# Chunk stage of a hybrid decoder layer: exponent arguments computed in three 32-row groups, four loaded and two transposed chunks, output transposes in another place

## The chip, the cores and the metric

The kernel runs on one core of a Trainium2 chip. The metric is device time in microseconds (us) of one execution. Lower is better. Each number quoted as "the time" is the median of three runs. The trace is of one further execution, taken with the hardware profiler.

## The reference, cut to what matters

Two layers (`DEPTH = 2`) of a decoder trunk with 1024 tokens and width 1024. Each layer has one input projection, three mixers that read it (mLSTM, sparse attention, Mamba-2 SSD), one output projection, and a SwiGLU FFN. The change concerns the stage that computes the mLSTM and the SSD mixer. Their recurrences are, per chunk of tokens:

```
# mLSTM, 4 heads of 64
log_d = where(causal, b[t] - b[s] + i[s], -inf)
s   = (q @ k.T) * exp(log_d - m_t)
num = s @ v + scale * (q @ C);  den = sum(s) + scale * (q @ n)
h   = num / max(|den|, exp(-m_t))
C   = decay * C + (w * k).T @ v ;  n = decay * n + sum(w * k)

# SSD, 8 heads of 64, state 128, 2 groups
seg    = where(causal, acum[t] - acum[s], -inf)
scores = (C_t @ B_s.T) * exp(seg)
y      = scores @ (x * dt) + (C @ state) * exp(acum)
state  = state * exp(a_last) + B.T @ (w * x * dt)
out    = rms_norm((y + d_skip * x) * silu(z))          # per group of 256
```

All operands are float32.

## The kernel before, in words

The kernel walks over the chunk stage in NT = 8 chunks of P = 128 tokens, in each of the two layers. All five engines run hand-written instruction lists, one block for each engine, and every ordering between engines is a semaphore wait (`pe.wait_ge(*rowed(...))`). There is no scheduler: the order in the source is the order on each engine, and a waiting instruction holds everything behind it on its engine.

A chunk c goes through these steps. The names are those of the code.

1. SP loads 20 tiles of 128x128 (1280 KB) from DRAM into `wc[c % 3]`. For c >= 3 it waits until chunk c-3 is wholly finished (`chunk_done`).
2. PE transposes 14 of these tiles into PSUM banks 0, 1, 2 and 0 again (`turns`, 4+4+4+2 tiles). ACT copies each bank into `rw` or `vaug` (`rows`), three places deep. The transposes wait until the exponentials of chunk c-1 have been read out of the same banks (`m_exp`, `s_exp`).
3. PE computes the arguments of the 12 exponentials (8 SSD heads, 4 mLSTM heads), `arguments`. For each of three banks there is one 128x512 bf16 matmul, which writes the causal mask, and then four selection matmuls that spread a row of `arow` (8 rows used) or `mrow` (4 rows used) over 128 partitions. A float32 matmul is two instructions in the trace, so `x8` in a row means four matmuls. The three banks go one after the other, and each ends with its own signal.
4. ACT takes 8 exponentials into `pss` and 4 into `pm` (`exps`). Both tiles exist once. So the exponentials of chunk c+1 wait until PE has used those of chunk c (`m_num`, `s_y`).
5. PE computes the products q.k and B.C (`products`), the contributions of the states (`m_inter`, `s_inter`), the updates of the states (`m_upd`, `s_upd`), and the two sums over a chunk (`m_num`, `s_y`). DVE combines them, updates the states and normalises. POOL scales the transposed rows.
6. The finished 128x768 output is transposed back (`turn_m` two tiles, `turn_s` four tiles), one chunk late: PE does it for chunk c-1 in the iteration of chunk c. ACT and DVE split it into the high and low halves `act_hi` and `act_lo` (`hi`, `lo`), which the next stage reads.

In `products` the q.k matmuls take rows 0-63 for one head and rows 64-127 for the next, and write two different banks. The banks for the q.k sums, the outputs and the rest alternate by chunk (`swing`).

In the input projection, long before this stage, ACT writes `arow` from a PSUM bank (`gate_rows`). The stage after it is the output projection. It begins in a new block, when all engines are through the chunk stage.

Of the kernel before, what the change touches and what calls it, by code (L numbers as in the profile page):

```python
# [30 lines left out]
P = 128  # L31
# [5 lines left out]
PLACES = 3  # L37
assert (NT - 2) % PLACES == 0
HALF = 512
HD = 64  # L40
# [56 lines left out]
def constant_table():  # L97
# [11 lines left out]
    for h in range(8):  # L109
        t[h, K_SEL + P * h:K_SEL + P * (h + 1)] = 1.0  # L110
# [10 lines left out]
def build(nc, x, positions, norm_w, w_in, gate_b, m_norm_w, conv_w, conv_b, dt_bias, a_log, d_skip, s_norm_w,  # L121
# [6 lines left out]
    with ctx:  # L128
# [71 lines left out]
        rw = [bb(f"rw{s}", [P, 12, P]) for s in range(PLACES)]  # L200
        vaug = [bb(f"vaug{s}", [P, MH, HD + 1]) for s in range(PLACES)]
# [160 lines left out]
        for L in range(DEPTH):  # L362
# [38 lines left out]
            with nc.Block() as block:  # L401
# [92 lines left out]
                def _(act):  # L494
# [693 lines left out]
            b_clear = sig("b_clear", PLACES + 2)  # L1188
            chunk_done = sig("chunk_done", NT)
# [7 lines left out]
            args = sig("args", 3 * NT)  # L1197
# [28 lines left out]
            hi_s = sig("hi_s", NT)  # L1226

# [20 lines left out]
            x_rows = lambda c: heads(rw[c % PLACES][:, 0:4, :].rearrange("p a b -> p (a b)"), HD)  # L1248
            flat = lambda a: a.rearrange("p a b -> p (a b)")

            with nc.Block() as block:
                @block.sync
                def _(sp):
# [5 lines left out]
                    for c in range(PLACES, NT):  # L1259
                        sp.wait_ge(*chunk_done(L, c - PLACES + 1))  # L1260
                        sp.dma_start(wc[c % PLACES][:, :, :], by_token[:, :, c * P:(c + 1) * P]).then_inc(chunk_in[c % PLACES].sem, 16)

                @block.gpsimd
                def _(pool):
                    for s in range(PLACES):
# [4 lines left out]
                    for c in range(NT):  # L1270
                        s = c % PLACES
# [21 lines left out]
                def _(pe):  # L1293
                    pe.wait_ge(*b_clear(L, PLACES + 2))

                    def turns(c):

                        w = wc[c % PLACES]
                        pe.wait_ge(*chunk_in[c % PLACES](L, 16 * (c // PLACES) + 16))
                        for b, js in enumerate(((0, 1, 2, 3), (4, 5, W_MK, W_MK + 1), (8, 9, 10, 11), (W_MV, W_MV + 1))):  # L1300
                            if b == 0 and c:
                                pe.wait_ge(*m_exp(L, c))
                            if b in (1, 2) and c:
                                pe.wait_ge(*s_exp(L, 2 * c - 2 + b))
                            if b == 3:
                                pe.wait_ge(*rowed(L, 4 * c + 1))
                            for i, j in enumerate(js):
                                mm = pe.transpose(bank(b % 3)[:, i * P:(i + 1) * P], w[:, j], ident)
                            mm.then_inc(turned.sem, 1)

                    def arguments(c):
# [3 lines left out]
                        for b in range(3):  # L1315
                            pe.wait_ge(*rowed(L, 4 * c + (2, 3, 4)[b]))
                            dst = bank((1, 2, 0)[b])
                            pe.matmul(dst.rearrange("p (h n) -> p h n", n=P), below[:, :], four(unit_b[:, :] if b < 2 else minus_b[:, :]),
                                      start=True, stop=False)
                            for h in range(4):  # L1320
                                if b < 2:
                                    mm = pe.matmul(dst[:, h * P:(h + 1) * P], cst[0:SH, K_SEL + P * (4 * b + h):K_SEL + P * (4 * b + h + 1)],
                                                   arow[0:SH, now], start=False, stop=(h == 3))
# [670 lines left out]
```

## Time and profile before

| what | value |
|---|---|
| time, median of 3 runs | 3206.84 us (3204.69 to 3207.92) |
| profiled execution, its own time | 3207.77 us |
| span from first to last instruction of it | 3206.0 us |
| PE busy | 2945.3 us, 92% of the span, 13396 matmul instructions |
| DVE busy | 1238.8 us, 39% |
| ACT busy | 913.0 us, 28% |
| POOL busy | 923.5 us, 29% |
| mean granted TensorE clock | 0.943 |
| DMA | 207.15 MB, mean 65 GB/s |

The kernel is bound by PE over most of its span. The shares are averages over stages of different kinds: projections and FFN are long rows of 128x512 matmuls at full clock, and the chunk stage is a net of short instructions on all engines. The granted clock is told in parts of 2.4 GHz, and takes the levels 1.00 (2.4 GHz) and 0.50 (1.2 GHz); a value in between is a mean over the stretch. Busy PE is not PE at its peak, since a matmul that streams 64 columns counts as busy just as one that streams 512.

### The profile page before, as it was taken

The page shows a single profiled execution, that of the slowest core. Times are in us where ns is not written, and L with a number is a line of the kernel's source. Part 1 is how long each engine was busy: PE and PEld are TensorE (multiplying, and loading weights), DVE is VectorE, ACT ScalarE, POOL GpSimd, SP SyncE. Part 2 cuts the span into 40 slices and gives each one's busy share as a digit, 9 for nine tenths or more (in the row PEclk, how much of TensorE's full clock was granted, in tenths as well). Part 3 has the DMA queues.
Part 4 walks back from the last instruction along what each step waited for, and adds up shares of the span by engine and source line. Part 5 has one row for each costly group of instructions (what it writes and reads, how often), then busy time and mean ns, then how long its engine had stood idle before and what let it go on. Part 6 is the DMA issues. An engine that isn't in the chain of part 4 may idle for free. (4 is left out here: it accounts for less than half of the span.)

```text
span 3206.0 us, 34381 instructions
## 1 busy us (share of the span) xinstructions
PE 2945.3 (92%) x13396; PEld 2351.7 (73%) x13396; DVE 1238.8 (39%) x2196; ACT 913.0 (28%) x1588; POOL 923.5 (29%) x470
## 2 busy tenths in 40 slices
PE   2999999897899999999939999998888999999997
PEld 1767877775778888888727678777667788888885
DVE  3359964463302111221333599545532111122114
ACT  3235434343311111111232354344432111111112
POOL 0127510223123223322311375103231322332223
PEclk9999999777999999999959999998789999999998
DMA  5102310323211111111241023103232111111113
GB/s 183 34 20 63 109 60 14 86 66 118 74 52 53 39 46 46 53 52 39 102 123 34 23 70 110 55 14 96 57 125 68 58 40 46 46 53 52 39 48 123
DMA packets 234143, 207.15 MB, mean 65 GB/s; under 512 B 20448, under 2 KB 208864, under 8 KB 233840
## 3 DMA queue, kind: packets, MB, share of 16 engines
q1 hardware_dynamic: 228272, 184.69, 19.0%
q10 hardware_dynamic: 5760, 20.97, 1.7%
q8 instruction: 70, 1.15, 0.1%
q14 instruction: 41, 0.34, 0.0%
HBM read 166.85 MB, written 42.99 MB: 65 GB/s over the span
## 5 line engine op out<-in xcount | busy, mean ns | idle before, releaser
L1910 PE MATMUL ps<-act_hi,whi 128*128 128x512 f32 x1408 | 552.0, 392 | 19.8 <-POOL wlo L1817 14.5
L1910 PE MATMUL ps<-act_lo,whi 128*128 128x512 f32 x1408 | 551.3, 392 | 0.0
L1910 PE MATMUL ps<-act_hi,wlo 128*128 128x512 f32 x1408 | 551.0, 391 | 0.0
L1944 DVE TENSOR_TENSOR hf<-sg,ps 128x1024 f32<-128x1024 f32 x44 | 53.7, 1221 | 931.7 <-PE ps L1910 931.7
L757 PE MATMUL ps<-act_hi,whi 128*128 128x512 f32 x960 | 395.2, 412 | 5.5 <-DVE act_lo L956 4.7
L757 PE MATMUL ps<-act_lo,whi 128*128 128x512 f32 x960 | 377.8, 394 | 0.0
L757 PE MATMUL ps<-act_hi,wlo 128*128 128x512 f32 x960 | 377.5, 393 | 0.0
L1129 DVE TENSOR_SCALAR_CACHE_REDUCE ties<-score,kth 128x384 uint8<-128x384 f32 (+5 forms) x396 | 348.4, 943 | 4.8
L1817 POOL TENSOR_TENSOR wlo<-raw,whi 128x1024 fp32r<-128x1024 f32 x84 | 200.3, 2396 | 499.6 <-ACT whi L1854 499.6
L1910 PEld LDWEIGHTS ps<-act_hi,whi 128*128 128x128 f32 x1408 | 266.5, 189 | 77.1 <-issue 21.4
L1950 DVE TENSOR_TENSOR yacc<-yacc,ps 128x1024 f32<-128x1024 f32 x176 | 214.8, 1220 | 264.1 <-PE ps L1924 264.1
L1910 PEld LDWEIGHTS ps<-act_lo,whi 128*128 128x128 f32 x1408 | 266.5, 189 | 56.0
L1910 PEld LDWEIGHTS ps<-act_hi,wlo 128*128 128x128 f32 x1408 | 266.3, 189 | 55.8
L1924 PE MATMUL ps<-dhi,hhi 128*128 128x512 f32 x704 | 276.5, 393 | 12.8 <-POOL dlo L1817 11.7
L1924 PE MATMUL ps<-dhi,hlo 128*128 128x512 f32 x704 | 276.0, 392 | 0.0
L1924 PE MATMUL ps<-dlo,hhi 128*128 128x512 f32 x704 | 276.0, 392 | 0.0
L458 POOL TENSOR_TENSOR wlo<-raw,whi 128x1024 fp32r<-128x1024 f32 x58 | 142.2, 2451 | 462.6 <-ACT whi L504 462.6
L1860 ACT ACTIVATE sg<-ps 128x1024 f32<-128x1024 f32 x44 | 45.1, 1026 | 738.2 <-PE ps L1910 738.2
L757 PEld LDWEIGHTS ps<-act_hi,whi 128*128 128x128 f32 x960 | 182.2, 190 | 85.7 <-issue 41.9
L757 PEld LDWEIGHTS ps<-act_hi,wlo 128*128 128x128 f32 x960 | 182.2, 190 | 39.9
L757 PEld LDWEIGHTS ps<-act_lo,whi 128*128 128x128 f32 x960 | 182.5, 190 | 35.4 <-issue 1.9
L1822 POOL TENSOR_TENSOR hlo<-hf,hhi 128x1024 fp32r<-128x1024 f32 x44 | 105.6, 2401 | 356.4 <-ACT hhi L1864 356.4
(289 smaller groups left out, 4115.1 us busy)
## 6 DMA issues: line engine op xcount, KB each, us to landing
raw<-in_w_in SPq DMA_DIRECT2D x56, 512.0 KB, 3.8
raw<-in_w_gate SPq DMA_DIRECT2D x44, 512.0 KB, 3.7
raw<-in_w_up SPq DMA_DIRECT2D x44, 512.0 KB, 3.8
raw<-in_w_down SPq DMA_DIRECT2D x44, 512.0 KB, 3.5
proj_scratch<-stage ACTq DMA_DIRECT2D x40, 512.0 KB, 2.7
wc<-proj_scratch SPq DMA_DIRECT2D x16, 1280.0 KB, 6.5
tap<-out SPq DMA_DIRECT2D x16, 512.0 KB, 3.5
xres<-out SPq DMA_DIRECT2D x16, 512.0 KB, 3.4
```

The costliest lines, as they stand in the source:

```text
L458: pool.tensor_tensor(wlo[u % 2][:, :], src, whi[u % 2][:, :].bitcast(F32), ALU.subtract)\
L757: mm = pe.matmul(ps[:, half, :], w[:, k], a[:, k, cols], start=(k == 0 and m == 0), stop=(k == KT - 1 and m == 2))
L1129: v.tensor_scalar(tie(c), of(c), at(kth, c), 0.0, op, ALU.add, accum_out=at(held, c))
L1817: pool.tensor_tensor(lo_t[s][:, :], raw[s][:, :], hi_t[s][:, :].bitcast(F32), ALU.subtract)\
L1822: pool.tensor_tensor(hlo[p][:, j], hf[:, :], hhi[p][:, j].bitcast(F32), ALU.subtract).then_inc(h_lo.sem, 1)
L1860: act.activation(sg[:, :], unit_psum(0), ACT.Silu).then_inc(silu.sem, 1)
L1910: mm = pe.matmul(ps[:, 2 * s + half, :], w[:, k], a[:, k, cols], start=(k == 0 and m == 0), stop=(k == KT - 1 and m == 2))
L1924: mm = pe.matmul(ps[:, 4 + 2 * (t % 2) + half, :], h[p][:, j, rows], w[j][:, cols], start=(j == 0 and m == 0), stop=(j == 1 and m == 2))
L1944: v.tensor_tensor(hf[:, :], sg[:, :], unit_psum(1), ALU.mult).then_inc(hidden.sem, 1)
L1950: v.tensor_tensor(yacc[:, t], yacc[:, t], turn_bank(t), ALU.add).then_inc(y_add.sem, 1)
```

## The change

- `PLACES = 4`: four chunks are loaded ahead instead of three. The load of chunk c waits for `gated` of chunk c-4, which is the last reader of `wc`, in place of `chunk_done`. `ROWS = 2`: the transposed rows `rw` and `vaug` have two places instead of three.
- The arguments of a chunk: `arow` now holds the SSD rows twice (partitions 0-7 and 32-39) and the mLSTM rows at partitions 64-67. The selection constants lie at the same three offsets. The three mask matmuls come first, then twelve selection matmuls that go round the three banks and the three row groups. There is one signal at the end instead of three. ACT writes the two extra copies once in each layer, in `gate_rows`.
- The transposes of chunk c+1 use two banks (0 and 1) instead of three, and are split: 8 tiles after `s_inter`, 6 tiles after `m_num`. Bank 2 takes the SSD output transposes (`turn_s`), which now stand between them, ahead of the last 6 tiles and of `s_y`, instead of after the arguments.
- ACT and DVE follow the new order: `to_hi_s` between the second and third row copy, `to_hi_m` last, `to_lo_s` after the update of the SSD state and ahead of the mLSTM sum.

```diff
-PLACES = 3
+PLACES = 4
+ROWS = 2
...
-        t[h, K_SEL + P * h:K_SEL + P * (h + 1)] = 1.0
+        for r0 in (0, 32, 64):
+            t[r0 + h, K_SEL + P * h:K_SEL + P * (h + 1)] = 1.0
...
                     def gate_rows():
+                        act.activation(arow[32:32 + SH, :], bank[0:SH, :], ACT.Copy)
                         act.activation(arow[0:SH, :], bank[0:SH, :], ACT.Copy).then_inc(aux_free[s].sem, 1)
                         act.wait_ge(*rows_v(L, 11))
+                        act.activation(arow[64:64 + MH, :], mrow[0:MH, :], ACT.Copy)
...
-                        sp.wait_ge(*chunk_done(L, c - PLACES + 1))
+                        sp.wait_ge(*gated(L, c - PLACES + 1))
...
-                    def turns(c):
+                    def turns(c, b):
...
+                        if b == 0 and c:
+                            pe.wait_ge(*m_exp(L, c))
+                        if b == 1 and c:
+                            pe.wait_ge(*s_exp(L, 2 * c - 1))
+                        if b >= 2:
+                            pe.wait_ge(*rowed(L, 4 * c + b - 1))
+                        for i, j in enumerate(js):
+                            mm = pe.transpose(bank(b % 2)[:, i * P:(i + 1) * P], w[:, j], ident)
...
-                        for b in range(3):
-                            pe.wait_ge(*rowed(L, 4 * c + (2, 3, 4)[b]))
...
+                        pe.wait_ge(*rowed(L, 4 * c + 4))
+                        if c >= 2:
+                            pe.wait_ge(*lo_s(L, c - 1))
+                        for b in (1, 2, 0):
+                            pe.matmul(tiles(bank(b)), below[:, :], four(unit_b[:, :] if b else minus_b[:, :]), start=True, stop=False)
+                        for h in range(4):
+                            for b, r0, n, k in ((1, 0, SH, h), (2, 32, SH, 4 + h), (0, 64, MH, h)):
+                                mm = pe.matmul(bank(b)[:, h * P:(h + 1) * P], cst[r0:r0 + n, K_SEL + P * k:K_SEL + P * (k + 1)],
+                                               arow[r0:r0 + n, now], start=False, stop=(h == 3))
+                        mm.then_inc(args.sem, 1)
...
                     def turn_s(c, b):
                         pe.wait_ge(*s_out(L, c + 1))
-                        pe.wait_ge(*gated(L, c + 1))
+                        if c + 1 < NT:
+                            pe.wait_ge(*s_exp(L, 2 * c + 4))
...
-                        if c:
-                            pe.wait_ge(*chunk_done(L, c - 1))
+                        if c >= 2:
+                            pe.wait_ge(*gated(L, c - 1))
...                                                     # after s_inter
+                        if c + 1 < NT:
+                            load_in(c + 1)
+                            turns(c + 1, 0)
+                            turns(c + 1, 1)
...                                                     # after turn_m
-                        if c + 1 < NT:
-                            turns(c + 1)
...                                                     # after m_num
+                        if c:
+                            turn_s(c - 1, 2)
+                        if c + 1 < NT:
+                            turns(c + 1, 2)
+                            turns(c + 1, 3)
...                                                     # after s_y
                             arguments(c + 1)
-                        if c:
-                            turn_s(c - 1, near)
...                                                     # ACT, after finish(c - 1)
-                            rows(c + 1)
+                            rows(c + 1, 0)
+                            rows(c + 1, 1)
                         if c:
-                            hi(c - 1, swing(c)[0])
+                            to_hi_s(c - 1)
+                        if c + 1 < NT:
+                            rows(c + 1, 2)
+                            rows(c + 1, 3)
+                        if c:
+                            to_hi_m(c - 1)
...                                                     # DVE, after the update of smem
+                        if c:
+                            to_lo_s(c - 1)
...                                                     # DVE, last in the iteration
-                            lo(c - 1, near)
+                            to_lo_m(c - 1)
```

PE's list in the middle of the chunk stage, one iteration, before. Here `cst,wc` are the transposes of loaded tiles, `cst,catr` those of outputs, `pss`, `pm` the exponentials, and the last eight rows are the arguments, `turn_s` and the products:

```order
L1381 MATMUL ps<-vaug,wk 128x130 x2
L1386 MATMUL ps<-xw,rw 128x256 x2
L1350 MATMUL ps<-cst,catr 128x128 x2
L1308 MATMUL ps<-cst,wc 128x128 x14
L1396 MATMUL ps<-vaug,pm 128x65 x4
L1402 MATMUL ps<-xdt,pss 128x64 x8
L1318 MATMUL ps<-unit_b,below 128x512
L1322 MATMUL ps<-arow,cst 128x128 x4
L1318 MATMUL ps<-unit_b,below 128x512
L1322 MATMUL ps<-arow,cst 128x128 x4
L1318 MATMUL ps<-minus_b,below 128x512
L1325 MATMUL ps<-mrow,cst 128x128 x4
```

The same place on PE with the change (the line numbers are those of the changed kernel, L1314 the transposes of loaded tiles, L1353 `turn_m`, L1362 `turn_s`):

```order
L1314 MATMUL ps<-cst,wc 128x128 x8
L1391 MATMUL ps<-vaug,wk 128x130 x2
L1396 MATMUL ps<-xw,rw 128x256 x2
L1353 MATMUL ps<-cst,catr 128x128 x2
L1404 MATMUL ps<-vaug,pm 128x65 x4
L1362 MATMUL ps<-cst,catr 128x128 x4
L1314 MATMUL ps<-cst,wc 128x128 x6
L1415 MATMUL ps<-xdt,pss 128x64 x8
L1325 MATMUL ps<-unit_b,below 128x512 x2
L1325 MATMUL ps<-minus_b,below 128x512
L1328 MATMUL ps<-arow,cst 128x128 x12
```

Eight transposes moved ahead of the state updates. `turn_s` moved from behind the arguments to ahead of the last six transposes. The three pairs of mask and selection matmuls became one run of three and one run of twelve.

ACT's list between the finish of a chunk and the next exponentials, before (L1467 writes the normalised SSD output, L1427 are the copies of the transposed rows, L1474 and L1476 the high halves of mLSTM and SSD, L1437 the SSD exponentials):

```order
L1467 ACTIVATE catr<-y,small 128x256 x2
L1427 ACTIVATE rw<-ps 128x512 x3
L1427 ACTIVATE vaug<-ps 128x4x64
L1474 ACTIVATE act_hi<-catf 128x2x128
L1476 ACTIVATE act_hi<-ps 128x4x128
L1437 ACTIVATE pss<-ps,scol_minus 128x128 x8
```

The same place on ACT with the change (L1474 the normalised output, L1437 the row copies, L1484 and L1480 the high halves of SSD and mLSTM, L1445 the exponentials):

```order
L1474 ACTIVATE catr<-y,small 128x256 x2
L1437 ACTIVATE rw<-ps 128x512 x2
L1484 ACTIVATE act_hi<-ps 128x4x128
L1437 ACTIVATE rw<-ps 128x512
L1437 ACTIVATE vaug<-ps 128x4x64
L1480 ACTIVATE act_hi<-catf 128x2x128
L1445 ACTIVATE pss<-ps,scol_minus 128x128 x8
```

The high half of the SSD output moved from the last place before the exponentials to a place among the row copies.

## Rows read from the trace of the kernel before

**Rows 1.** Windows: both chunk stages, then one period of layer 1 and of layer 0.

```profile
core 0: us, PE busy (x) PEld busy (x) DVE busy (x) ACT busy (x) POOL busy (x), PEclk, DMA share, GB/s
572.40:731.30 158.90, 139.31 (x792) 115.92 (x792) 86.95 (x199) 68.10 (x225) 40.55 (x45) 0.75 0.28 73
2167.00:2319.80 152.80, 131.06 (x792) 109.71 (x792) 87.55 (x199) 67.76 (x225) 40.46 (x43) 0.80 0.28 76
2192.22:2206.32 14.10, 14.10 (x98) 12.25 (x97) 9.74 (x24) 7.98 (x27) 4.89 (x5) 0.88 0.00 1
614.88:634.15 19.27, 18.07 (x101) 14.83 (x101) 10.76 (x26) 8.25 (x28) 4.89 (x5) 0.73 0.26 69
```

**Rows 2.** Timeline (start, us, what): first mask matmul of chunks 0 and 7, both layers.

```profile
581.90 0.63 PE L1318 MATMUL ps<-unit_b,below 128*128 128x512 bf16 x1
...
708.90 0.38 PE L1318 MATMUL ps<-unit_b,below 128*128 128x512 bf16 x1
...
2176.79 0.38 PE L1318 MATMUL ps<-unit_b,below 128*128 128x512 bf16 x1
...
2296.34 0.38 PE L1318 MATMUL ps<-unit_b,below 128*128 128x512 bf16 x1
```

**Rows 3.** Timeline of PE, chunk 1 to 2 of layer 1.

```profile
2200.59 0.61 PE L1381 MATMUL ps<-vaug,wk 128*128 128x130 f32 x4
2201.04 1.03 PE L1386 MATMUL ps<-xw,rw 128*128 128x256 f32 x4
...
2202.12 1.73 PE L1308 MATMUL ps<-cst,wc 128*128 128x128 f32 x14
2203.69 1.00 PE L1396 MATMUL ps<-vaug,pm 128*128 128x65 f32 x8
2204.53 1.95 PE L1402 MATMUL ps<-xdt,pss 128*128 128x64 f32 x16
2206.32 0.38 PE L1318 MATMUL ps<-unit_b,below 128*128 128x512 bf16 x1
2206.63 1.15 PE L1322 MATMUL ps<-arow,cst 8*128 8x128 f32 x8
...
2210.52 0.89 PE L1358 MATMUL ps<-cst,catr 128*128 128x128 f32 x4
```

**Rows 4.** PE's waits (total us, times, longest), chunk stage of layer 0, then 1.

```profile
PE ps L1308 <- DMA wc<-proj_scratch: 14.5, 6, 7.6
...
PE ps L1308 <- DMA wc<-proj_scratch: 14.9, 6, 8.3
```

**Rows 5.** Timeline of PE, selections and q.k products of chunk 2, layer 0.

```profile
618.99 2.07 PE L1325 MATMUL ps<-mrow,cst 4*128 4x128 f32 x8
...
622.04 1.23 PE L1337 MATMUL ps<-wc 64*128 64x128 f32 x8
```

**Rows 6.** Windows with the clock at either level, layer 0.

```profile
600.00:609.00 9.00, 9.00 (x38) 7.46 (x38) 3.70 (x9) 5.09 (x20) 0.32 (x1) 0.50 0.00 0
610.00:613.00 3.00, 3.00 (x27) 2.82 (x26) 1.66 (x5) 1.68 (x4) 1.25 (x2) 1.00 0.00 0
```

**Rows 7.** Timeline of ACT, layer 1, exponentials and the normalised SSD output.

```profile
2229.42 2.16 ACT L1437 ACTIVATE pss<-ps,scol_minus 128x128 f32<-128x128 f32 x8
2231.42 1.20 ACT L1443 ACTIVATE pm<-ps,gcol 128x128 f32<-128x128 f32 x4
...
2234.25 0.91 ACT L1467 ACTIVATE catr<-y,small 128x256 f32<-128x256 f32 x2
```

**Rows 8.** Timeline of DVE, layer 1, low half and the next products.

```profile
2229.56 0.69 DVE L1521 TENSOR_TENSOR act_lo<-ps,act_hi 128x512 fp32r<-128x512 f32 x1 [2.42 <-ACT act_hi L1476]
2231.62 1.29 DVE L1533 TENSOR_TENSOR pss<-pss,ps 128x512 f32<-128x512 f32 x2 [1.37 <-ACT pss L1437]
```

**Rows 9.** Timeline of ACT, layer 0, the copy of `arow` in the projection.

```profile
145.12 1.02 ACT L658 ACTIVATE arow<-ps 8x1024 f32<-8x1024 f32 x1 [0.82 <-PE ps L798]
...
150.78 0.60 ACT L548 ACTIVATE stage<-ps 128x512 f32<-128x512 f32 x1 [4.55 <-PE ps L757]
```

More of the change, by code:

```diff
@@ L1226, in build @@
             hi_s = sig("hi_s", NT)
+            lo_s = sig("lo_s", NT)
             U_WO = N_PROJ
@@ L1264, in _ @@
                 def _(pool):
-                    for s in range(PLACES):
+                    for s in range(ROWS):
                         pool.memset(vaug[s][:, :, HD:HD + 1], 1.0).then_inc(b_clear.sem, 1)
@@ L1314, in arguments @@
                         four = lambda a: a.rearrange("p (o n) -> p o n", o=1).broadcast_to([P, 4, P])
-                        for b in range(3):
-                            pe.wait_ge(*rowed(L, 4 * c + (2, 3, 4)[b]))
[L1317 to L1323, printed above, removed]
-                                else:
-                                    mm = pe.matmul(dst[:, h * P:(h + 1) * P], cst[0:MH, K_SEL + P * h:K_SEL + P * (h + 1)],
-                                                   mrow[0:MH, now], start=False, stop=(h == 3))
-                            mm.then_inc(args.sem, 1)
+                        pe.wait_ge(*rowed(L, 4 * c + 4))
[8 more added lines that the diff above has]
+                        mm.then_inc(args.sem, 1)
                     def products(c):
@@ L1359, in turn_s @@
                         mm.then_inc(cat_s.sem, 1)
-                    turns(0)
+                    load_in(0)
+                    for b in range(4):
+                        turns(0, b)
                     arguments(0)
@@ L1412, in _ @@
                     turn_m(NT - 1, near)
-                    turn_s(NT - 1, 7)
+                    pe.wait_ge(*lo_s(L, NT - 1))
+                    turn_s(NT - 1, 2)
                 @block.scalar
@@ L1469, in finish, with to_hi_m, to_hi_s @@
                         ins.then_inc(s_out.sem, 1)
-                    def hi(c, b):
-                        now = slice(c * P, (c + 1) * P)
+                    def to_hi_m(c):
                         act.wait_ge(*gated(L, c + 1))
-                        act.activation(act_hi[:, 0:2, now], catf[:, :, :], ACT.Copy).then_inc(hi_m.sem, 1)
+                        act.activation(act_hi[:, 0:2, c * P:(c + 1) * P], catf[:, :, :], ACT.Copy).then_inc(hi_m.sem, 1)
+                    def to_hi_s(c):
                         act.wait_ge(*cat_s(L, c + 1))
-                        act.activation(act_hi[:, 4:8, now], tiles(bank(b)), ACT.Copy).then_inc(hi_s.sem, 1)
-                    rows(0)
+                        act.activation(act_hi[:, 4:8, c * P:(c + 1) * P], tiles(bank(2)), ACT.Copy).then_inc(hi_s.sem, 1)
+                    for b in range(4):
+                        rows(0, b)
                     for c in range(NT):
@@ L1519, in lo, with to_lo_s @@
                         v.tensor_tensor(act_lo[:, 0:2, now], catf[:, :, :], act_hi[:, 0:2, now].bitcast(F32), ALU.subtract)
+                    def to_lo_s(c):
+                        now = slice(c * P, (c + 1) * P)
                         v.wait_ge(*hi_s(L, c + 1))
-                        v.tensor_tensor(act_lo[:, 4:8, now], tiles(bank(b)), act_hi[:, 4:8, now].bitcast(F32), ALU.subtract)\
-                         .then_inc(chunk_done.sem, 1)
+                        v.tensor_tensor(act_lo[:, 4:8, now], tiles(bank(2)), act_hi[:, 4:8, now].bitcast(F32), ALU.subtract)\
+                         .then_inc(lo_s.sem, 1)
                     for c in range(NT):
-                        s = c % PLACES
+                        s = c % ROWS
                         near, far = swing(c)
```

64 lines of the change are left out of this document (26 added, 38 removed).

## The prediction

> **What bounds the kernel now.** I read the page first (PE busy 92%), and then went to the stage that the change touches, by windows of time, since the share is a mean over unlike stages. The two chunk stages take 158.9 and 152.8 us of the span [rows 1], together 311.7 us or 10%. The reader is to see three things there: PE is busy 86 to 88% of it, DVE 55 to 57%, ACT 43 to 44%, so PE is the bound; and PE has a granted clock of 0.75 and 0.80, where the whole span has 0.943. Second, from the starts of the first mask matmul of chunks 0 and 7 the period of a chunk is (708.90 - 581.90)/7 = 18.1 us in layer 0 and (2296.34 - 2176.79)/7 = 17.1 us in layer 1 [rows 2], 17.6 in the mean. Third, PE waits for the loads of `wc`: 14.5 and 14.9 us in 6 waits each [rows 4]. One of the six is the start of the stage (7.6 and 8.3); the five others are 6.9 and 6.6 us.
>
> PE's own work in a period at full clock: the shortest period, 2192.22 to 2206.32, has PE busy all its 14.10 us at a mean clock of 0.88 [rows 1]. So 0.24 of it, 3.4 us, ran at half the clock, which cost 1.7 us, and 12.4 is left; it is the one period without `turn_s`, which adds 0.5. Sum 12.9. The parts of it, from start to start [rows 3]: `m_upd` 0.45 (0.55 where it doesn't follow closely), `s_upd` 0.87, `turn_m` 0.21, 14 transposes 1.57, `m_num` 0.84, `s_y` 1.79, the arguments 2206.32 to 2210.52 = 4.20; products and state contributions are the rest, 2.5. The mean period is 17.6, so 4.7 us go to the low clock and to waits, 0.96 of them (13.5/14) to the `wc` loads.
>
> The low clock is tied to the arguments. The granted clock is 0.50 from 600 to 609 and 1.00 from 610 to 613 [rows 6]. It falls while PE works through selections that use 8 or 4 of the 128 rows, and within a period never in a stretch of transposes and full-row products. In most chunks it falls during or just behind the selections, and stays low through the products and state contributions.
>
> **The change part by part.**
>
> *Arguments.* Before: three times a mask (0.31) and eight selection instructions (1.09, that is 8 x 0.112 and a gap of 0.2 [rows 3]; the third bank as the first). Now the eight of one bank run beside the eight of the other two, if row groups run side by side. What the trace shows of that: at the low clock eight selections on the same rows take 2.07 us, and the eight q.k instructions, alternating between rows 0-63 and 64-127 and between two banks, take 1.23 for the same 128 columns each [rows 5]. Less the tail of one instruction (0.4 to 0.5) that is 0.21 and 0.11 for each: pairs run fully side by side. For three groups I take the same: 8 rounds x 0.112 = 0.87. Masks: 0.31 + 2 x 0.22 = 0.75 (512 bf16 columns, no change of rows between them). Exit 0.2. Sum 1.8 against 4.2 at full clock: 2.4 us less. Bounds: not side by side at all, 24 x 0.109 + 0.2 + 0.75 = 3.6 (0.6 less); below 1.8 nothing, since one group's 0.87 must pass.
>
> The Trainium skill (TensorE: Matmul & The Clock Gate, "Measured speedup vs the span model") gives 3.07x for four row tiles rather than 4x. By this share three groups give 2.3x, an estimate of 1.14 us in place of 0.87, and the whole time would be some 4 us longer than by the row. I stay with the row, and the range has room for the other.
>
> *Clock.* The stretch of few-row work shrinks from 3 x 1.09 with masks between them to one of 1.1 us. In layer 1 a stretch with one run of eight selections at its end (2204.5 to 2207.7: `s_y`, mask, selections) kept full clock (those selections take 1.15 us [rows 3], against 2.07 at the low clock [rows 5]). So I expect the clock to stay at 1.00 from about the second chunk on. Bounds: mean clock as now (0.78), or 1.00.
>
> The Trainium skill says of PE transposes (same page, "Part 4: PE-mode transpose") that the full clock "doesn't engage" for them. By that rule the change, which puts more transposes next to the selections, would lose clock; but 610 to 613 holds the 14 transposes and stands at 1.00 [rows 6], so the measurement speaks against it. What it would give is the second rival.
>
> *Loads of `wc`.* Chunk c is asked for when chunk c-4 is gated, that is more than a period before PE needs it, and lands in 6.5 us (page, part 6): the 13.5 us of waits go. The fourth load stands ahead of two weight loads that are needed only in the next stage: nothing. The first chunk still has to land.
>
> *Two banks for the transposes.* At the start of the stage banks 2 and 3 of the turn must wait for row copies of 0.6 each (the 128x512 copy in [rows 9] is of this shape), and the arguments wait for all four copies: 0.8 us later per layer.
>
> *Copies in `gate_rows`.* Two of 1.02 us, behind them ACT is idle 4.55 us [rows 9]. Nothing; without that cover 2 us per layer.
>
> *The new period.* With PE faster, the ring through ACT decides. From the end of the arguments: signal 0.1; twelve exponentials 2.0 + 1.2 = 3.2 [rows 7]; then eight transposes, which wait for them, 0.95 (DVE is done with `pm` at about the same time: 2.2 for the SSD exponentials, then 1.2 for its products [rows 8] and 0.7 for the two half as long); then on PE without a wait `m_upd` 0.55, `s_upd` 0.87, `turn_m` 0.21, `m_num` 0.84, `turn_s` 0.5, six transposes 0.67, `s_y` 1.79 = 5.4; arguments 1.8; semaphores 0.2. Sum 11.7. The SSD output that `turn_s` needs is ready 5.9 us in (2229.42 to 2235.16 is 5.7 [rows 7]), ahead of `turn_s` at about 7.1. PE alone needs 12.9 - 2.4 = 10.5 and is idle 1.2 us. DVE is busy 10.76 us in a period [rows 1] and now waits in `to_lo_s` for ACT's high half, about 0.6 us, with the mLSTM sum and its eight followers queued behind: 11.4. Two rings that nearly tie make each other late, so I take 11.9. Bounds: DVE's busy time alone, 10.8 or rounded 11.0; above, 13.0 with the 3.07x rule and a lost microsecond.
>
> *Sum.* Stage now: 9.5 to the first arguments (581.90 - 572.40) + 0.8; seven periods 83.3; a clock that is low in the first chunk 1.0; from the last arguments to the end 19.5 (now 731.3 - 708.9 = 22.4 and 23.5; the arguments there save 3.3, and the rest of it, a chain through DVE and ACT, stays). Together 114.1 us. Saved 158.9 - 114.1 = 44.8 and 152.8 - 114.1 = 38.7, in all 83.5 us. The profiled execution took 3207.8 (span 3206.0 and 1.8 around it): 3207.8 - 83.5 = 3124.3. It lies 0.9 above the median of the runs shown, so 3123.4; rounded 3124.
>
> **The rivals.**
>
> *First: three groups don't run side by side.* The trace shows two halves only, not thirds, and the selections have 8 and 4 rows. Then arguments cost 3.6, PE's work is 12.3, the ring is 13.5, and the clock falls as now, which takes 0.6 more: 14.1 (the shortest period of today [rows 1]). 14 x (17.6 - 14.1) = 49, less 1 at the start: 3160.
>
> *Second: side by side, but the clock goes on falling in each chunk.* For it: the waits of PE in the new ring (1.2 us) and more transposes; against it: [rows 6]. With the clock of today, 0.78, PE's 10.5 become 13.5, and with the wait, which shortens, 14.3 at most: 14 x 3.3 = 46 saved, 3161; with 0.88 it is 10.5/0.88 + 1.2 = 13.1, 63 saved, 3144.
>
> *Third, the other side: slower.* If the idle time in the ring keeps the clock at 0.50 through the stage, PE's list is 2 x 10.5 less what doesn't scale (`s_y` and `m_num`, bound by loading weights, about 2.6) = 18.4, and with what is left of the wait 18.8: 14 x (18.8 - 17.6) = 17 longer, 3224. It decides once the period is over 17.6, a mean clock under about 0.55. Against it: even today's chunks with 1.4 us of wait for `wc` come back to 1.00.
>
> *Fourth: a new wait eats the gain.* A load or the single signal of the arguments (ACT used to start after the first bank, 2.8 us ahead of the third) holds ACT. The signal is in the ring above already; only a wait of 5 us per chunk would take the gain, and I find none.
>
> **How the numbers follow.** Forecast 70%, its own range 3108 (period 11.0, 12.6 us less, and 3 more in the ends) to 3140 (period 13.0). First rival 9% (3150 to 3170), second 14% (3140 to 3165), slower 4%, no change 3%. The range reaches from 3108 to 3158 and leaves out about 2 in 10. A measurement of this kernel tells 0.2% (6.4 us) from no change: faster 0.93, same 0.03, slower 0.04.
>
> **What would show it.** Stages of about 114 us each, at a clock near 0.95; a period of 11.9. The selections as one run of 24 instructions in 1.1 to 1.2 us at full clock. No wait of PE for `wc` but the first. Waits of PE for ACT's `pm` of about 1 us in each chunk, and DVE waiting about 0.6 us for `act_hi` of the SSD. It would be wrong if the 24 instructions take over 2.5 us, if the clock in the stage stays under 0.9, or if PE waits over 1 us for `lo_s` or the row copies ahead of the masks.

## The result and the profile after

| | before | changed |
|---|---|---|
| time, us (median of 4 runs) | 3207.01 (3204.69 to 3207.92) | 3123.11 (3122.56 to 3123.50) |
| ratio, 95% interval | | 0.9739 [0.9724, 0.9753] |
| span of the profiled execution | 3206.0 | 3121.3 |
| granted clock over the span | 0.943 | 0.954 |

The changed kernel is 84 us faster. From the head of its page: PE's busy time fell, its share stayed at 92%, and the work of the other engines is as before. (One run of one kernel below, at 3408 us with a granted clock of 0.83 over its span, is left out of that kernel's median.)

```profile
PE 2857.1 (92%) x13396; PEld 2280.2 (73%) x13396; DVE 1243.5 (40%) x2196; ACT 916.2 (29%) x1592; POOL 921.2 (30%) x468
```

The windows of both chunk stages and of one period (they answer to [rows 1]; columns as there):

```profile
573.20:684.70 111.50, 89.48 (x792) 75.78 (x792) 87.91 (x199) 67.20 (x225) 39.20 (x42) 0.93 0.40 105
2119.40:2235.00 115.60, 93.40 (x792) 78.89 (x792) 88.15 (x199) 67.44 (x225) 39.41 (x44) 0.88 0.38 101
618.41:630.31 11.90, 10.88 (x101) 9.29 (x99) 11.18 (x26) 8.24 (x28) 4.86 (x6) 1.00 0.40 106
```

The stages took 158.9 and 152.8 us and take 111.5 and 115.6: 47.4 + 37.2 = 84.6, the whole gain. What lies ahead of, between and behind them is unchanged to 1 us. In the period DVE is now busy 11.18 of 11.90 us and PE 10.88: the bound has moved from PE to DVE. The clock, 0.73 to 0.88 in the two periods of before, is 1.00 in this one. Over the stages it is 0.93 and 0.88, since it is low at their start and end.

The timeline of PE over one period of layer 0 (start, us; answers to [rows 3]):

```profile
611.48 1.06 PE L1314 MATMUL ps<-cst,wc 128*128 128x128 f32 x8 [0.88 <-ACT pm L1450]
612.67 0.71 PE L1391 MATMUL ps<-vaug,wk 128*128 128x130 f32 x4
613.23 1.03 PE L1396 MATMUL ps<-xw,rw 128*128 128x256 f32 x4
614.09 0.38 PE L1353 MATMUL ps<-cst,catr 128*128 128x128 f32 x2
614.31 1.00 PE L1404 MATMUL ps<-vaug,pm 128*128 128x65 f32 x8
615.15 0.61 PE L1362 MATMUL ps<-cst,catr 128*128 128x128 f32 x4
615.59 0.82 PE L1314 MATMUL ps<-cst,wc 128*128 128x128 f32 x6
616.25 1.90 PE L1415 MATMUL ps<-xdt,pss 128*128 128x64 f32 x16
617.98 0.59 PE L1325 MATMUL ps<-unit_b,below 128*128 128x512 bf16 x2
618.41 0.38 PE L1325 MATMUL ps<-minus_b,below 128*128 128x512 bf16 x1
618.72 1.17 PE L1328 MATMUL ps<-arow,cst 8*128 8x128 f32 x24
619.82 0.71 PE L1340 MATMUL ps<-wc 64*128 64x128 f32 x8
```

The arguments take 619.82 - 617.98 = 1.84 us, against 4.20 [rows 3]. The 24 selections take 1.10 from their start to the next instruction; less 0.2 of exit that is 0.90, eight rounds of 0.112. Their bar in the timeline is 1.17 long, where that of eight selections alone was 1.15 [rows 3]. The same holds at the low clock, which the first chunk of layer 1 shows: 2.08 for 24, where eight alone took 2.07 [rows 5].

```profile
2132.25 2.08 PE L1328 MATMUL ps<-arow,cst 8*128 8x128 f32 x24
```

PE now has two gaps: 0.88 us for ACT's `pm`, and about 0.3 between those eight transposes and `m_upd` (612.67 - 611.48 = 1.19, where the two follow each other at 0.90 in the second period, 599.92 to 600.82). The wait for `pm` is new, PE did not have it before; `wc` is now waited for once (waits of PE in layer 0: total, times, longest; the first line answers to [rows 4]):

```profile
PE ps L1314 <- DMA wc<-proj_scratch: 8.0, 1, 8.0
PE ps L1314 <- ACT pm L1450: 6.1, 7, 0.9
```

DVE and POOL over the same period, from their timelines:

```profile
611.87 0.75 DVE L1557 TENSOR_TENSOR pm<-pm,ps 128x256 f32<-128x256 f32 x2
...
616.42 0.69 DVE L1540 TENSOR_TENSOR act_lo<-ps,act_hi 128x512 fp32r<-128x512 f32 x1 [0.35 <-ACT act_hi L1484]
...
618.55 1.15 DVE L1591 TENSOR_TENSOR hsq<-nd 128x256 f32<-128x256 f32 x1
...
623.77 0.75 DVE L1557 TENSOR_TENSOR pm<-pm,ps 128x256 f32<-128x256 f32 x2
```

```profile
618.23 1.19 POOL L1285 TENSOR_TENSOR xdt<-rw,scol 128x512 f32<-128x512 f32 x1 [1.69 <-PE ps L1415]
```

DVE waits once, 0.35 us for `act_hi`, and from there to the end of the next `pm` it has no wait, only small gaps between instructions that need each other's result. One instruction is longer than its like: the square `hsq` (two operands in SBUF) takes 1.15 us while POOL's product `xdt` runs beside it, and 0.42 where it does not (in the first and last chunk of each layer).

### The profile page after: what moved, and what is told of

Its sections match the earlier page's. It is cut to its first block and busy times, and to the rows that moved or that the text cites. A ratio compares the mean times of both kernels' runs of the same rounds, so it can differ in the third digit from the quotient of the medians.

```text
span 3121.3 us, 34397 instructions
## 1 busy us (share of the span) xinstructions
PE 2857.1 (92%) x13396; PEld 2280.2 (73%) x13396; DVE 1243.5 (40%) x2196; ACT 916.2 (29%) x1592; POOL 921.2 (30%) x468
## 3 DMA queue, kind: packets, MB, share of 16 engines
q8 instruction: 70, 1.15, 0.2%
## 5 line engine op out<-in xcount | busy, mean ns | idle before, releaser
L1932 PE MATMUL ps<-act_hi,whi 128*128 128x512 f32 x1408 | 551.9, 392 | 19.8 <-POOL wlo L1839 14.5
L1946 PE MATMUL ps<-dhi,hhi 128*128 128x512 f32 x704 | 276.5, 393 | 12.8 <-POOL dlo L1839 11.7
```

The costliest lines, as they stand in the source:

```text
L1932: mm = pe.matmul(ps[:, 2 * s + half, :], w[:, k], a[:, k, cols], start=(k == 0 and m == 0), stop=(k == KT - 1 and m == 2))
L1946: mm = pe.matmul(ps[:, 4 + 2 * (t % 2) + half, :], h[p][:, j, rows], w[j][:, cols], start=(j == 0 and m == 0), stop=(j == 1 and m == 2))
```

## The experiments

All times are medians; before stands for the unchanged kernel, run on the same chip in the same hours: 3206.07 us with the first four, 3202.53 with the next four, 3201.30 with the last four. Ratios are against it. "Period" is the time between first mask matmuls of adjacent chunks.

### The parts of the change apart

**Groups of rows alone.** The kernel before, with the 24 selections in one run on three row groups and one signal; its loads, order and banks are kept.

```diff
-for b in range(3):                     # a bank at a time, all on rows 0 to 7
+pe.wait_ge(*rowed(L, 4 * c + 4))
+for b in (1, 2, 0):
+    pe.matmul(tiles(bank(b)), below[:, :], four(...), start=True, stop=False)
+for h in range(4):
+    for b, r0, n, k in ((1, 0, SH, h), (2, 32, SH, 4 + h), (0, 64, MH, h)):
+        mm = pe.matmul(..., cst[r0:r0 + n, ...], arow[r0:r0 + n, now], ...)
```

> The kernel before, with the arguments in three row groups alone (three loads ahead, order of transposes and outputs as before). Theory (fewer microseconds of few-row work, and so a clock that stays high): arguments 1.8 us in place of 4.2, granted clock of the chunk stages about 0.9, the wait for wc of 1 to 1.5 us per chunk stays, period about 14.3 us, time about 3160 us. Rival (the clock gain comes from the new order of the instructions, the grouping saves only its own 2.4 us per period): clock about 0.78, period 15.2 or more, time 3173 us or more.

Measured: 3155.51 us, ratio 0.9841 [0.9825, 0.9858]. 

```profile
592.00:697.00 105.00, 82.40 (x721) 68.63 (x719) 81.76 (x184) 57.98 (x196) 35.55 (x37) 1.00 0.24 64
```

The clock stays at 1.00 without the new order (0.78 in the kernel before, same window). PE is busy only 78% of that window. This part alone gives 50 us, and PE now waits more: in layer 0 16.7 us for `wc` (14.5 before) and 10.5 us in 7 waits for DVE's `pm` ahead of `m_upd` (1.1 in 3 before).

**Loads alone.** Four places for `wc`, two for its rows, and SP asks for a chunk once chunk c-4 is gated.

```diff
-PLACES = 3
+PLACES = 4
+ROWS = 2
-sp.wait_ge(*chunk_done(L, c - PLACES + 1))
+sp.wait_ge(*gated(L, c - PLACES + 1))
```

> The kernel before, with four loaded chunks, two transposed ones and the load released by gated. Theory: the waits for wc after the first, 13.5 us in all, go, the clock goes on falling in each chunk (0.75 to 0.80): time about 3191 us. Rival (the waits only hid another wait, for row copies or exponentials): 3204 to 3207 us.

Measured: 3188.94 us, ratio 0.9943 [0.9927, 0.9960]: 17 us. PE waits for `wc` only at the start of the stage. The clock goes on falling in each chunk: 0.82 in the window below, where the kernel before has 0.76, and 0.80 for 0.83 in layer 1 (2180 to 2300).

```profile
584.00:700.00 116.00, 113.80 (x708) 96.50 (x707) 75.63 (x170) 54.59 (x183) 35.93 (x36) 0.82 0.28 76
```

**Everything but the row groups.** The changed kernel, with all 24 selections on rows 0 to 7.

```diff
-for b, r0, n, k in ((1, 0, SH, h), (2, 32, SH, 4 + h), (0, 64, MH, h)):
-    mm = pe.matmul(..., cst[r0:r0 + n, ...], arow[r0:r0 + n, now], ...)
+for b, src, n, k in ((1, arow, SH, h), (2, arow, SH, 4 + h), (0, mrow, MH, h)):
+    mm = pe.matmul(..., cst[0:n, ...], src[0:n, now], ...)
```

> The changed kernel, with all twelve selections on rows 0 to 7 (arow) and 0 to 3 (mrow), in the same order over the banks. Theory (the row groups run side by side, and that is what the gain rests on): the run of 24 selection instructions takes 24 x 0.11 = 2.6 us in place of 1.1, the clock falls again in most chunks, period 14 to 14.5, time 3155 to 3160 us. Rival (going round three banks is what makes them quick): no change, 3123 us. Rival (the clock stays high, only the work is longer): period 13.2, time 3142 us.

Measured: 3158.15 us, ratio 0.9847 [0.9830, 0.9863]. Its steady period (641.60 to 655.41) is filled by PE, at a clock of 0.88:

```profile
641.60:655.41 13.81, 13.81 (x102) 12.44 (x102) 11.29 (x26) 8.24 (x28) 5.03 (x5) 0.88 0.35 93
642.34:645.21 2.87, 2.87 (x25) 2.75 (x25) 2.77 (x4) 0.00 (x0) 0.69 (x1) 1.00 0.85 209
646.00:649.00 3.00, 3.00 (x13) 2.82 (x12) 1.67 (x4) 2.97 (x14) 0.00 (x0) 0.50 0.00 0
649.30:650.50 1.20, 1.20 (x12) 1.17 (x11) 1.20 (x4) 1.10 (x6) 0.92 (x1) 1.00 0.00 0
```

The selections, 2.87 us from 642.34 to 645.21, run at full clock; it falls just behind them, although PE never stops, and is back when the eight transposes begin (649.33). With loads and order in place, the row groups are worth 35 us.

### Is it the clock, and what lowers it?

**Selections over all 128 rows, in the kernel before.** `arow` and `mrow` are cleared below their rows, and each selection reads 128 rows in place of 8 or 4: the same number of instructions and columns, the same result, every row of the array in use. (POOL clears the two tiles once per layer, in the projection.)

```diff
-pe.matmul(dst[...], cst[0:SH, ...], arow[0:SH, now], ...)
+pe.matmul(dst[...], cst[:, ...], arow[:, now], ...)
```

> The kernel before, with its selections over all 128 rows: rows that were left out are zero in the constants, and the row tiles are cleared first (two POOL memsets per layer). The number of instructions, columns and their order stay. Theory (the clock falls because the selections use 8 or 4 rows of 128): granted clock in the chunk stages 0.9 or more, no fall behind the arguments, period 16.0 to 16.3, time 3185 to 3190 us. Rival (it falls for the length of the instructions, the waits or the transposes): clock 0.75 to 0.80 as before, time 3207 to 3211 us.

Measured: 3171.62 us, ratio 0.9886 [0.9870, 0.9903], 34 us faster for more rows per matmul.

```profile
584.00:700.00 116.00, 95.98 (x743) 85.45 (x743) 79.59 (x179) 60.46 (x207) 38.06 (x39) 1.00 0.28 77
```

In the same window the kernel before has 0.76. Layer 1 agrees but for one fall: 0.98 from 2180 to 2270, for 0.83 before. That fall, 0.50 from 2227 to 2229, came behind two waits of PE, 1.74 us for DVE's `pm` and 2.19 for `wc`, with 1.8 us of work between them. So the cause of the falls in each chunk is shown: selections that use few rows bring the clock down.

The size was too low in every theory, 17 to 22 us for 34, and not all of the 34 is the clock. At full clock the arguments take 628.56 - 625.24 = 3.32 us here and 4.20 before [rows 3]: the gaps between the mask (128 rows) and the selections (8 or 4 rows) are gone.

```profile
625.24 0.38 PE L1322 MATMUL ps<-unit_b,below 128*128 128x512 bf16 x1
...
628.56 0.60 PE L1362 MATMUL ps<-cst,catr 128*128 128x128 f32 x4
```

That is 0.88 us in each of 16 chunks, up to 14 us (an estimate; the other waits of PE shift too). The expectation left this term out, and what remains, about 20, lies within it.

**The same in the new order.** Everything but the row groups, with selections over 128 rows.

```diff
-mm = pe.matmul(..., cst[0:n, ...], src[0:n, now], ...)
+mm = pe.matmul(..., cst[:, ...], src[:, now], ...)
```

> same_rows with its selections over all 128 rows (the left-out rows are zero, the row tiles are cleared first). Theory (same_rows lost by two things: 1.5 us more of selections per chunk, and a falling clock): the clock stays at 1.00 after the start, the run takes 2.7 us, period about 13.1, time about 3140 us. Rival (the clock plays no part in the loss): 3156 to 3160 us.

Measured: 3141.74 us (median of the three runs left), ratio 0.9810 [0.9778, 0.9841]; period 13.12 at a clock of 1.00. So the 35 us of the row groups are about 19 for running side by side (3141.74 against 3123; 23 by the ratios) and about 16 for the clock (3158.15 against 3141.74; 12 by the ratios). Here the arguments differ little: 3.42 us from the first mask to the products, against 3.61 on few rows. So at most 3 of the 16 are the shorter run, and this pair is the cleaner test of what the clock costs.

**Three row groups, one bank after the other.** The groups stay, but the eight instructions of one stand together.

```diff
-for h in range(4):
-    for b, r0, n, k in ((1, 0, SH, h), (2, 32, SH, 4 + h), (0, 64, MH, h)):
+for b, r0, n, k0 in ((1, 0, SH, 0), (2, 32, SH, 4), (0, 64, MH, 0)):
+    for h in range(4):
```

> The changed kernel, its three row groups kept, but the four selections of one bank and group are issued before those of the next. Theory (matmuls start in the order of the list, so groups run side by side only where neighbours in the list are of different groups): the run of 24 instructions takes about 2.6 us as on the same rows, and the time is that of same_rows, 3155 to 3160 us. Rival (PE looks far enough ahead to start a later group early): 1.1 to 1.5 us, time 3123 to 3129 us.

Measured: 3142.01 us, ratio 0.9813 [0.9788, 0.9838]. Neither theory: the run of 24 lies between (PE's timeline).

```profile
649.16 2.26 PE L1329 MATMUL ps<-arow,cst 8*128 8x128 f32 x24
651.36 0.71 PE L1341 MATMUL ps<-wc 64*128 64x128 f32 x8
```

2.20 us to the next instruction less 0.2 of exit is 2.0, 18 rounds of 0.112 where one after the other takes 24 and side by side 8: as if six of the 24 had overlapped, which would be three at each of the two changes of group (the trace does not show the single ones). On these rows, then, instructions of different groups run side by side where they alternate, and mostly not where eight of one group stand together. The bank alternates along with the group; alternating banks alone is not enough (2.87 us with all on the same rows), and whether groups would run side by side into one bank was not tested. The clock falls again in some periods, behind the longer run:

```profile
640.00:660.00 20.00, 20.00 (x145) 17.87 (x144) 17.14 (x38) 13.76 (x49) 8.90 (x9) 0.85 0.25 67
```

### What sets the new period

The prediction named a ring through arguments, exponentials and PE (11.7) and put DVE behind it (11.4). The trace after suggests DVE. The ring was forecast at 11.7 and taken as 11.9, which is also what was measured, so the time can't tell them apart; other kernels can.

**A mask matmul twice.** 0.22 us more of PE inside the ring through the arguments; DVE's ring goes through another part of PE's list, ahead of which PE has a gap. The extra one writes what the next overwrites.

```diff
+pe.matmul(tiles(bank(1)), below[:, :], four(unit_b[:, :]), start=True, stop=True)
 for b in (1, 2, 0):
```

> The changed kernel, with the mask of bank 1 written twice, 0.22 us more on PE ahead of the selections of each chunk. Theory A (the period is set by a ring through DVE: products with the exponentials, mLSTM update and sum, SSD output, and the arguments have 0.3 us to spare, since PE waits that long for DVE's pm after its transposes): 3123 to 3124.5 us. Theory B, that of the prediction (the ring goes through the arguments and the exponentials): 16 x 0.22 = 3.5 us longer, 3126.5 us.

Measured: 3122.46 us, ratio 0.9754 [0.9733, 0.9776]. The period did not move: first masks of adjacent chunks at 617.80 and 629.70 are 11.90 apart (PE's timeline).

```profile
617.80 0.38 PE L1324 MATMUL ps<-unit_b,below 128*128 128x512 bf16 x1
...
623.42 1.06 PE L1314 MATMUL ps<-cst,wc 128*128 128x128 f32 x8 [0.90 <-ACT pm L1451]
624.40 0.71 PE L1392 MATMUL ps<-vaug,wk 128*128 128x130 f32 x4
...
629.70 0.38 PE L1324 MATMUL ps<-unit_b,below 128*128 128x512 bf16 x1
```

From the eight transposes to `m_upd` (L1392) it is now 0.98 us, against 1.19: the gap has taken the extra matmul. In these periods the ring through the arguments does not decide. In the second period of each layer, 11.56 in the changed kernel, it does: there the mask shows in full, 11.78.

**POOL's `xdt` later.** POOL forms `xdt` after fading `smem`, away from `hsq`: 5.6 us behind the first mask in place of 0.25. Nothing else changes.

```diff
-if c:
-    pool.wait_ge(*s_y(L, c))
-pool.tensor_tensor(xdt[...], x_rows(c), gate_of(scol, c, 3, SH, HD), ALU.mult)...
 pool.wait_ge(*s_inter(L, c + 1))
 ...                                    # fade of smem
+if c:
+    pool.wait_ge(*s_y(L, c))
+pool.tensor_tensor(xdt[...], x_rows(c), gate_of(scol, c, 3, SH, HD), ALU.mult)...
```

> The changed kernel, with POOL's product xdt moved behind the fade of the SSD state. In the changed kernel DVE's square hsq takes 1.15 us instead of 0.42 in each period, while POOL works on xdt. Theory A (DVE sets the period, and a DVE instruction with two operands in SBUF is held up by the POOL product beside it): hsq goes back to 0.42 and the period falls by 0.3, where the ring through the arguments takes over: 3118 to 3120 us, less if another DVE instruction is held up instead. Theory B (the arguments set the period): 3123 us, no change, although hsq is shorter.

Measured: 3119.34 us, ratio 0.9742 [0.9720, 0.9764], period 11.57 (619.69 to 631.26). From the timeline:

```profile
619.69 0.59 PE L1325 MATMUL ps<-unit_b,below 128*128 128x512 bf16 x2
620.26 0.42 DVE L1591 TENSOR_TENSOR hsq<-nd 128x256 f32<-128x256 f32 x1
621.74 2.18 ACT L1445 ACTIVATE pss<-ps,scol_minus 128x128 f32<-128x128 f32 x8 [2.57 <-PE ps L1328]
623.95 1.28 DVE L1552 TENSOR_TENSOR pss<-pss,ps 128x512 f32<-128x512 f32 x2 [0.30 <-ACT pss L1445]
625.09 1.06 PE L1314 MATMUL ps<-cst,wc 128*128 128x128 f32 x8 [0.89 <-ACT pm L1450]
625.15 0.75 DVE L1557 TENSOR_TENSOR pm<-pm,ps 128x256 f32<-128x256 f32 x2
625.30 1.04 POOL L1290 TENSOR_TENSOR xdt<-rw,scol 128x512 f32<-128x512 f32 x1
625.81 0.81 DVE L1523 TENSOR_TENSOR catr<-nd,small 128x256 f32<-128x256 f32 x1
625.99 0.67 PE L1391 MATMUL ps<-vaug,wk 128*128 128x130 f32 x4
631.26 0.59 PE L1325 MATMUL ps<-unit_b,below 128*128 128x512 bf16 x2
```

`hsq` is back at 0.42, which frees 0.73 on DVE, and the period falls by only 0.33: DVE now waits 0.30 for ACT's `pss`. The hold has moved to `catr` (L1523, 0.81 for 0.48), which also reads two tensors of SBUF beside POOL.

**Both together.**

> xdt_later with the mask of bank 1 written twice. In the changed kernel that mask cost nothing (period 11.90 with and without). Theory A (with xdt later, the ring through the arguments decides and has nothing to spare): period 11.57 + 0.22 = 11.79, 3 us more than xdt_later. Rival (DVE, with the instruction that is now held up, still decides): period 11.57.

Measured: 3121.69 us, ratio 0.9750 [0.9736, 0.9763], period 11.78 (617.71 to 629.49). This is `xdt` later with the second mask. The extra 0.21 of PE shows in full: with `xdt` later the ring through the arguments decides, and its length is 11.57.

**Three places for `wc` in the changed kernel.**

```diff
-PLACES = 4
+PLACES = 3
```

> The changed kernel with three places for loaded chunks instead of four. Theory (what removed the waits is the earlier release by gated, not the fourth place): the load is asked for at the gate, 7.9 us before PE is through with waiting for the exponentials (615.47 to 623.37 in the changed kernel), and lands in 6.5, so the period stays 11.90 and the time 3123 us. Rival (the fourth place is needed): a wait for wc of over 0.5 us per chunk, 3128 us or more.

Measured: 3122.77 us, ratio 0.9755 [0.9738, 0.9772], period 11.89, and one wait for `wc`, the first (7.9). The fourth place brings nothing here: asking for the load at the gate is enough.

**The bank that is free first, first.** On top of `xdt` later, PE first transposes into bank 1, whose exponentials are done before those of bank 0.

```diff
-js = ((0, 1, 2, 3), (4, 5, W_MK, W_MK + 1), (8, 9, 10, 11), (W_MV, W_MV + 1))[b]
+js = ((4, 5, W_MK, W_MK + 1), (0, 1, 2, 3), (8, 9, 10, 11), (W_MV, W_MV + 1))[b]
-mm = pe.transpose(bank(b % 2)...)
+mm = pe.transpose(bank(1 - b % 2)...)
```

> xdt_later, and the first four transposes of the next chunk go to bank 1, which is free after the first four exponentials, instead of bank 0, which is free after the last; the second four to bank 0. Theory A (the ring through the arguments decides: twelve exponentials, eight transposes, five groups on PE, arguments): four transposes, 0.45 us, leave the ring, and the period falls from 11.57 until DVE decides, whose instructions take 10.8 and one of which is held up 0.4: 11.2 to 11.3, time 3114 to 3116 us. Rival (DVE decides already): 11.57, no change against xdt_later.

Measured: 3118.85 us, ratio 0.9744 [0.9731, 0.9758]. Expected were 3114 to 3116 and a period of 11.2 to 11.3; the period is 11.56, as without the swap.

```profile
622.54 0.66 PE L1314 MATMUL ps<-cst,wc 128*128 128x128 f32 x4 [0.36 <-ACT pm L1450]
...
623.49 0.71 PE L1391 MATMUL ps<-vaug,wk 128*128 128x130 f32 x4 [0.29 <-DVE pm L1557]
```

The wait for ACT's `pm` shrinks from 0.89 to 0.36, and a wait of 0.29 for DVE's `pm` stands behind it. In the kernel with `xdt` later DVE's `pm` ended at 625.15 + 0.75 = 625.90 and `m_upd` began at 625.99: two paths from the exponentials to `m_upd` that tied, of which the swap shortened one. The other, through DVE's `pss` and `pm`, is as long as before, and DVE waits 0.30 for ACT's `pss` in both kernels.

**The changed kernel once more**, in the same hours as the last three, as a yardstick.

> The changed kernel once more, as the measure for the three beside it on the same chip: 3122 to 3124 us, period 11.90.

Measured: 3123.47 us (3118.69 to 3123.98), ratio 0.9756 [0.9742, 0.9770], span 3122.0. The version with `xdt` later and the swap (3118.85, 3117.28 to 3121.46, span 3119.7) has the lowest median, 4.6 us under this; by the ratios `xdt` later alone is as good (0.9742 against 0.9744). The periods account for 3.4 us of it: ten of the fourteen are shorter, by 0.34, and the second of each layer was 11.56 already. The intervals of the ratios overlap, so the time alone does not establish a gain; the periods do.

## Why the prediction was right, and where it was not

*The number.* 3124.0 was forecast, 3123.11 measured. The sum, term by term: 83.5 us saved in the stages against 84.6.

| term, us | forecast | layer 0 | layer 1 |
|---|---|---|---|
| start to first arguments | 10.3 | 10.5 | 11.5 |
| seven periods, with the low clock in the first | 84.3 | 81.9 | 85.0 |
| last arguments to the end | 19.5 | 19.1 | 19.1 |
| stage | 114.1 | 111.5 | 115.6 |

(Layer 0: first masks of chunks 0 and 7 at 583.69 and 665.57; layer 1: 2130.86 and 2215.85.) In both layers the last five of the seven periods are 11.90, as forecast, and the second is 11.56. The first is 10.83 in layer 0, where the clock is at 1.00 from the first arguments on, and 13.94 in layer 1, where it is at 0.50 until 2139. The forecast had 12.9 for it in both; with the later start of layer 1, that is 2.6 us too much in one stage and 1.5 too little in the other, and the two errors nearly cancel, which is luck. The first period is not even the same from one execution to the next: the changed kernel once more has 11.45 in layer 1, and the one with `xdt` later has 13.97 in layer 0.

*Arguments, 4.2 to 1.8.* Right: 1.84. The three groups run fully side by side, 0.112 us a round. The share of 3.07 for four row tiles that the Trainium skill gives (TensorE: Matmul & The Clock Gate, "Measured speedup vs the span model"; measured there with 512 columns) is not what these selections of 128 columns show: eight rounds took 0.90, not 1.14. The first rival, 3160, assumed one after the other; with all selections on the same rows the time is 3158.15.

*Clock.* Right in cause, and here the experiments went beyond the trace: full rows in place of few remove the low stretch of each chunk. In the kernel before they give 34 us, some 20 of it by the clock (an estimate); in the new order the clock is worth 12 to 16. The second rival fell: 1.00 from the second chunk on, in both layers. Over the stages the mean is 0.93 and 0.88, below the 0.95 that was written down, since the low clock at start and end weighs more in a shorter stage. By the rule of the Trainium skill on transposes (same page, "Part 4: PE-mode transpose") the full clock would not come up for them; here it stays at 1.00 through the 20 transposes of each period, which stand among other matmuls; no run here has transposes alone.

*Loads.* Right: one wait for `wc` is left. 13.5 us of waits were to go; the loads alone give 17. But the fourth place is not what does it.

*Copies in `gate_rows`.* Right, hidden: ACT's timeline in layer 0 has the two further copies, and is idle 2.32 us behind them where it was 4.55 [rows 9].

```profile
145.67 1.02 ACT L659 ACTIVATE arow<-ps 8x1024 f32<-8x1024 f32 x1 [0.82 <-PE ps L801]
146.70 1.01 ACT L660 ACTIVATE arow<-ps 8x1024 f32<-8x1024 f32 x1
147.74 1.06 ACT L662 ACTIVATE arow<-mrow 4x1024 f32<-4x1024 f32 x1
...
151.34 0.60 ACT L549 ACTIVATE stage<-ps 128x512 f32<-128x512 f32 x1 [2.32 <-PE ps L760]
```

*The new period.* The number, 11.90, is right by luck, and the step behind it is wrong. The prediction said "the ring through ACT decides", 11.7, with DVE at 11.4, and took 11.9 because "two rings that nearly tie make each other late". The runs show that they do not: the longer one alone sets the period. The ring through the arguments is 11.57 (seen once DVE is out of the way, and it carries the extra mask in full); DVE's ring is 11.90 and does not feel that mask. DVE's ring can be added up from the rows above: from `act_lo` at 616.42 without a pause to the end of the first `pm` product at about 624.5, 8.1 us; from there through PE's `m_upd`, `s_upd`, `turn_m`, `m_num`, `turn_s`, 612.67 to 615.76, 3.1; ACT's `act_hi`, 0.6; signals 0.1. What the 11.4 lacked is the 0.73 us by which POOL's `xdt` holds `hsq`; its wait for `act_hi` was sized at 0.6 and is 0.35: 11.4 + 0.73 - 0.25 = 11.9. For `hsq` the trace of before gave no sign, since there it started just ahead of `xdt` wherever the two met, and it was POOL that took longer. But the hold itself was in that trace, on another product: in six of the sixteen chunks `catr`, which also reads two tensors of SBUF, takes 0.55 to 1.28 for 0.42 beside POOL's fade of `smem` (timelines of POOL and DVE, before, layer 0). Asking of each DVE product with two such operands what POOL will run beside it in the new order would have found the term.

```profile
644.83 1.06 POOL L1286 TENSOR_TENSOR smem<-smem,decs 128x512 f32<-128x512 f32 x1 [9.20 <-PE ps L1375]
644.98 1.19 DVE L1507 TENSOR_TENSOR catr<-nd,small 128x256 f32<-128x256 f32 x1
```

*Waits.* PE's wait of about 1 us for ACT's `pm` in each chunk is there, 0.88. It looks like the bound and is not: the swap of banks took most of it away and gained nothing.

*What stays open.* The parts overlap. Groups alone give 50 us, loads alone 17, and all together 84; what the order of work is worth alone was not run, only that order and loads together, without the groups, give 48. Why the first period of a layer has the low clock in some executions and not in others was not tested either.

## What to carry to other kernels

Selections that use few rows of the array cost twice here: their own time, and the clock of what follows. Put them on different row groups, next to each other in the program and alternating, or widen them to all rows if there is nothing to pair them with. Where two rings nearly tie, a single sum for the period says nothing about which of them holds; lengthen each by a known amount and look at which one the period follows. And before a wait is removed, look at what ends next behind it: here it was 0.09 us away.

## What the runs showed of the hardware

- Eight fp32 selections on each of three row groups (rows 0 to 7, 32 to 39, 64 to 67), alternating, take the time of eight: 24 in 1.10 us against 2.87 on the same rows. At the low clock 24 take 2.08 and eight alone 2.07. In runs of eight per group 24 take 2.20 at full clock, as if only six of them overlapped.
- The granted clock fell to 0.50 behind selections of 8 and 4 rows though PE did not stop, and did not fall behind the same instructions over 128 rows. From 584 to 700 of the span: 0.76 before, 1.00 with full rows. With full rows it fell once, in layer 1, behind waits of 1.74 and 2.19 us.
- A run of eight selections of 8 or 4 rows between full-row matmuls has gaps that go away with full rows: the arguments, three masks and 24 instructions, take 4.20 us on few rows and 3.32 on all, at full clock.
- A DVE product of two tensors in SBUF is held while POOL's 128x512 product runs beside it: 1.15 us for 0.42, ended 0.28 after POOL's. Where DVE started first (634.31 against 634.40 before), it took 0.43 and POOL 1.23 for 1.04. The Trainium skill has this contention with "two SBUF inputs" (GPSIMD Engine Reference, "Specifications"); its price here, the rest of POOL's instruction, is what decided the period.

Before, the two stood so (timeline of DVE and POOL, layer 0):

```profile
634.31 0.43 DVE L1570 TENSOR_TENSOR hsq<-nd 128x256 f32<-128x256 f32 x1
634.40 1.23 POOL L1282 TENSOR_TENSOR xdt<-rw,scol 128x512 f32<-128x512 f32 x1 [1.02 <-PE ps L1402]
```
